# A decoder step on one core: the first doubling level of a triangular inverse as VectorE products, and a new order of the steps around it

## Time and profile before

| | before |
|---|---|
| median of 3 runs | 1878.42 us (1875.55 to 1878.49) |
| the profiled execution | 1879.94 us, span 1878.2 us |
| TensorE busy, share of the span | 1542.3 us, 82% |
| VectorE busy | 648.0 us, 35% |
| ScalarE busy | 304.9 us, 16% |
| GpSimd busy | 63.6 us, 3% |
| bytes from HBM | 499.87 MB, 271 GB/s over the span |

### The profile page before, as it was taken

The page is one execution under the profiler, slowest core; times in us unless marked ns, Lnnn a source line. Parts: engine busy times, 40 slices in busy tenths (PEclk is TensorE's granted clock), DMA queues, the critical chain, the costliest instruction groups (busy, mean ns, idle before and its releaser), DMA issues.

```text
span 1878.2 us, 24556 instructions
## 1 busy us (share of the span) xinstructions
PE 1542.3 (82%) x8870; PEld 880.0 (47%) x8870; DVE 648.0 (35%) x1288; ACT 304.9 (16%) x704; POOL 63.6 (3%) x103
## 2 busy tenths in 40 slices
PE   7999999999999999999996675666757667576574
PEld 4676767676767676767752231222312223122121
DVE  6746565656565656410121120111201112010013
ACT  2323232323232323100112000000000000000012
POOL 1101010101010101000000000000000000000000
PEclk9999999999999999999997887888878888788787
DMA  7323232323232323374589999999999999999995
GB/s 286 109 100 113 92 120 82 120 82 120 82 120 82 120 82 120 110 292 165 204 373 426 429 426 429 429 428 428 429 428 427 429 429 429 427 429 430 428 403 212
DMA packets 71904, 510.35 MB, mean 272 GB/s; under 512 B 20496, under 2 KB 23696, under 8 KB 37808
## 3 DMA queue, kind: packets, MB, share of 16 engines
q1 hardware_dynamic: 71808, 509.60, 67.2%
q0 software_dynamic: 48, 0.12, 0.0%
HBM read 499.87 MB, written 9.82 MB: 271 GB/s over the span
## 4 chain that ended last, share of the span: by engine, by line
PE 41%; DMA 34%; DVE 16%; issue 4%; ACT 2%; SPq 1%; DVEq 1%; ACTq 0%
DMA arena<-w_up 22%; DVE arena L1424 16%; DMA arena<-w_down 12%; PE ps_PJ L723 11%; PE ps_C L1069 8%; PE ps_PJ L923 7%; ACT arena L1152 2%; SPq L560 1%; PE ps_C L1120 1%; PE ps_SB L1120 1%; PE ps_YB L1120 1%; PE ps_RT L1120 1%; PE ps_C L696 0%; PE ps_PJ L1023 0%; PE ps_SB L852 0%
## 5 line engine op out<-in xcount | busy, mean ns | idle before, releaser
L723 PE MATMUL ps_PJ<-arena 128*128 128x320 f32 x1792 | 536.6, 437 | 0.0
L1069 PE MATMUL ps_C<-arena 128*32 128x512 f32 x2048 | 285.1, 719 | 178.4 <-DMA arena<-w_gate 110.3
L723 PEld LDWEIGHTS ps_PJ<-arena 128*128 128x128 f32 x1792 | 324.7, 190 | 124.6 <-issue 17.9
L1424 DVE TENSOR_TENSOR arena<-arena,ps_PJ 128x512 f32<-128x512 f32 (+2 forms) x112 | 73.5, 657 | 614.7 <-PE ps_PJ L1023 495.3
L1069 PEld LDWEIGHTS ps_C<-arena 128*32 128x32 f32 x2048 | 79.3, 130 | 377.4 <-issue 375.0
L1152 ACT ACTIVATE arena<-arena 32x160 f32<-32x160 f32 (+9 forms) x350 | 146.6, 419 | 322.0 <-DVEq L422 134.7
L1424 DVE TENSOR_TENSOR arena<-arena 128x512 f32<-128x512 f32 (+12 forms) x311 | 161.8, 520 | 73.5 <-ACTq L422 41.2
L1152 ACT ACTIVATE arena<-ps_C 128x128 f32<-128x128 f32 (+3 forms) x68 | 27.4, 403 | 893.2 <-PE ps_C L1069 530.7
L923 PE MATMUL ps_PJ<-arena 128*128 128x320 f32 x512 | 142.4, 433 | 1.0 <-DVEq L422 1.0
L923 PEld LDWEIGHTS ps_PJ<-arena 128*128 128x128 f32 x512 | 95.5, 190 | 40.2 <-issue 3.3
L1424 DVE TENSOR_TENSOR arena<-ps_PJ,arena 128x512 f32<-128x512 f32 x32 | 22.1, 692 | 258.0 <-PE ps_PJ L1016 257.9
(11 more groups left out here) (181 smaller groups left out, 1175.7 us busy)
## 6 DMA issues: line engine op xcount, KB each, us to landing
arena<-w_down SPq DMA_DIRECT2D x64, 2048.0 KB, 21.5
arena<-w_gate SPq DMA_DIRECT2D x61, 2048.0 KB, 20.4
arena<-w_up SPq DMA_DIRECT2D x61, 2048.0 KB, 20.1
arena<-win SPq DMA_DIRECT2D x59, 1024.0 KB, 4.8
arena<-w_out SPq DMA_DIRECT2D x16, 1024.0 KB, 7.0
arena<-w_gate SPq DMA_DIRECT2D x6, 1024.0 KB, 8.0
arena<-xT SPq DMA_DIRECT2D x8, 640.0 KB, 7.4
arena<-s_ret SPq DMA_DIRECT2D x8, 512.0 KB, 3.8
```

What stands on the lines that cost most here:

```text
L723: last = mm(pj(j)[:, 0:T], wt[j % NSLOT][:, kt, :], hT[:, kt, :], start=kt == 0, stop=kt == KT - 1)
L1069: last = mm((GB, UB)[u][h * CAP:(h + 1) * CAP, :], xg[:, kt, h * CAP:(h + 1) * CAP], w[h](k), start=kt == 0, stop=kt == KT - 1)
L1424: ins = build(*args)
```

## The change

- Level 1 leaves TensorE. `k1`, `i1` and `j1` and their banks go. In their place `u0` does level 1 with VectorE products: with the mask of level 1 (`Am[0]`) and `Vc`, two row shuffles inside each group of four, two products and two additions on single columns and pairs of columns, and the sum of both. Then come the transposition and `spread` as before. `u0` now also waits for the first product of `am`.
- `am` on GpSimd does the mask of level 1 first, then the two masks of the short sequences, then levels 2 to 4. All six products now wait for `ax`; the counts of `lmk` follow.
- `us0` stands ahead of `u0`, in part 0 of tile q, instead of behind `cv` in part 1.
- The moves of ScalarE get names of their own, `mb`, `mx`, `mv`. `mb` stands where it stood; the others come later: `rqb` stands behind `k3 i3` and ahead of `mx`, `xv` on VectorE behind `j3` and `mv` behind the evacuation of tile kr.

```diff
 PLAN:
-    "q": "@v ax am -va u0 | cv us0 | | k1 i1 | zs1 xb | j1 pd | ds1 | k2 i2",
-    "kr": "@q | rqa j2 zs2 xk | | rqb k3 i3 | ds2 xv | j3 | | k4 i4",
-    "vr": "@kr | rka j4 rs0 | | rkb k5 i5 -pr | ts vt | j5 rs1 | tkk -pw |",
+    "q": "@v ax am -va us0 u0 | cv | | | zs1 xb mb | pd | ds1 | k2 i2",
+    "kr": "@q | rqa j2 zs2 xk | | k3 i3 rqb mx | ds2 | j3 xv | | k4 i4",
+    "vr": "@kr mv | rka j4 rs0 | | rkb k5 i5 -pr | ts vt | j5 rs1 | tkk -pw |",
 
 buffers:
+        rows4, pair4 = cut(3200, 128, c=NC), inv[:, 1536:1600].rearrange("p (g e) -> p g e", e=2)
 
 TensorE:
                 elif s[0] == "k":
-                    pe.wait_ge(inverse, 2 * (INNER * p + int(s[1])) - 1)
+                    pe.wait_ge(inverse, 2 * ((INNER - 1) * p + int(s[1]) - 1) - 1)
 ...
 ScalarE:
-                elif s in ("xb", "xk", "xv"):
-                    x = tok[:, "vbk".index(s[1]), :, :]
-                    act.wait_ge(done("tr"), 3 * p + 1 + "bkv".index(s[1]))
+                elif s in ("mb", "mx", "mv"):
+                    x = tok[:, ("mv", "mb", "mx").index(s), :, :]
+                    act.wait_ge(done("tr"), 3 * p + 1 + ("mb", "mx", "mv").index(s))
 ...
 VectorE, u0:
+            third_row = [i // 4 * 4 + 2 for i in range(32)]
+            second_row = [i // 4 * 4 + (1 if i % 4 == 0 else 2) for i in range(32)]
 ...
                     TT(Vc[:, :, :], Ac[:, :, :], inner[0][:, None, :].broadcast_to([P, NC, BK]), ALU.mult)
                     TT(Vc[:, :, :], Vc[:, :, :], unit[:, None, :].broadcast_to([P, NC, BK]), ALU.add)
+                    x1, v1, sx = by_four(Am[:, 0, :, :]), by_four(Vc), by_four(rows4)
+                    SHUF(rows4[:, :, :], Vc[:, :, :], third_row)
+                    dve.wait_ge(lmk, (INNER + 1) * p + 1)
+                    TT(pair4[:, :, 0:1], x1[:, :, 2:3], sx[:, :, 3:4], ALU.mult)
+                    TT(x1[:, :, 3:4], x1[:, :, 3:4], pair4[:, :, 0:1], ALU.add)
+                    SHUF(rows4[:, :, :], Am[:, 0, :, :], second_row)
+                    TT(pair4[:, :, :], sx[:, :, 2:4], v1[:, :, 1:2].broadcast_to([P, BK, 2]), ALU.mult)
+                    TT(x1[:, :, 2:4], x1[:, :, 2:4], pair4[:, :, :], ALU.add)
+                    TT(Vc[:, :, :], Vc[:, :, :], Am[:, 0, :, :], ALU.add)
                     TR(Uc.rearrange("p c j -> p (c j)"), Vc.rearrange("p c j -> p (c j)")).then_inc(inverse, 1)
                     spread(Ud, Uc).then_inc(inverse, 1)
 ...
 GpSimd, am:
                     wait_freed(pool, "g4", p)
+                    pool.wait_ge(done("ac"), 2 * p + 1)
+                    TT(Am[:, 0, :, :], Ac[:, :, :], inner[1][:, None, :].broadcast_to([P, NC, BK]), ALU.mult).then_inc(lmk, 1)
                     for k in range(1, 3):
                         TT(As[:, k - 1, :], GM[:, NC, 0:P], lvlT[k], ALU.mult).then_inc(lmk, 1)
-                    pool.wait_ge(done("ac"), 2 * p + 1)
-                    for k in range(1, INNER):
+                    for k in range(2, INNER):
                         TT(Am[:, k - 1, :, :], Ac[:, :, :], inner[k][:, None, :].broadcast_to([P, NC, BK]), ALU.mult).then_inc(lmk, 1)
```

More of the change, by code:

```diff
@@ L89 @@
 LATE = {"u1": 1, "s1": 2, "u2": 1, "r2": 2, "a2": 2, "s2": 2, "r3": 2, "a3": 2, "s3": 4, "mu": 3, "va": 7}
-UNSEEN = ("xb", "xk", "xv", "ts", "pk", "ck", "cr", "cv", "e3", "lo", "sq", "pc", "pe", "p1", "p2", "ps", "b1", "b1k", "b1l", "b2a", "b2b", "ax", "am", "u0", "us0", "vt", "mk", "pd", "pr", "pw", "rqa", "rqb", "rka", "rkb", "th", "mr", "mg", "my")
+UNSEEN = ("xb", "xk", "xv", "mb", "mx", "mv", "ts", "pk", "ck", "cr", "cv", "e3", "lo", "sq", "pc", "pe", "p1", "p2", "ps", "b1", "b1k", "b1l", "b2a", "b2b", "ax", "am", "u0", "us0", "vt", "mk", "pd", "pr", "pw", "rqa", "rqb", "rka", "rkb", "th", "mr", "mg", "my")
 def schedule(now, late):
@@ L761, in step @@
                     k = int(s[-1])
-                    pe.wait_ge(lmk, (INNER + 1) * p + k)
+                    pe.wait_ge(lmk, (INNER + 1) * p + 1 + k)
                     if k == 1:
@@ L777, in step @@
                     k = int(s[1])
-                    pe.wait_ge(inverse, 2 * (INNER * p + k))
+                    pe.wait_ge(inverse, 2 * ((INNER - 1) * p + k - 1))
                     if k < INNER:
@@ L1258, in step @@
                     last.then_inc(done("ac"), 1)
-                elif s in ("k1", "k2", "k3", "k4"):
+                elif s in ("k2", "k3", "k4"):
                     wait_filled(act, s, p)
@@ L1441, in _, with by_four @@
             swapped = [i ^ 1 for i in range(32)]
+            third_row = [i // 4 * 4 + 2 for i in range(32)]
+            second_row = [i // 4 * 4 + (1 if i % 4 == 0 else 2) for i in range(32)]
+            def by_four(x):
+                return x.rearrange("p c (g e) -> p (c g) e", e=4)
             FILL(eps[:, 0:1], NORM_EPS)
@@ L1616, in step @@
                     TR(Us, V[:, NC, :]).then_inc(done("us"), 1)
-                elif s in ("i1", "i2", "i3", "i4"):
+                elif s in ("i2", "i3", "i4"):
                     wait_filled(dve, s, p)
                     spread(Zd, bank(s)[:, 0:P].rearrange("p (b j) -> p b j", b=NB32)).then_inc(free(s), 1)
-                elif s in ("j1", "j2", "j3", "j4"):
+                elif s in ("j2", "j3", "j4"):
                     wait_filled(dve, s, p)
```

## The result

| | before | after |
|---|---|---|
| median of the runs | 1876.94 us (16 runs) | 1881.12 us (16 runs) |
| after over before | | 1.0025, 95% interval 1.0017 to 1.0032 |
| profiled execution, span | 1879.94 us, 1878.2 us | 1880.7 us, 1878.9 us |

A forecast was written before the change was run, and what follows sets the result against it. The chain through VectorE and ScalarE from `@v` to `i4` bounds the pair loop: +1.58 - 0.97 = +0.61 us a pair, +4.6 us over 7.5 pairs on the 1878.42 us median. Forecast 1883.0 us, range 1873 to 1888.

The forecast's parts named there:

- The chain, not TensorE, sets the time: From `@v` to `i4`, VectorE and ScalarE set each pair's time, now 21.52 us; TensorE's work there is filler.
- TensorE's saving lost at `j2`: TensorE's own work shrinks 1.49 us a pair, but it then waits some 2.3 us at `j2` for ScalarE.
- First part, `@v` to the end of `xb`: VectorE's stretch up to `xb`: 7.73 us in place of 6.15, 1.58 longer.
- meetings: VectorE products colliding with GpSimd's, 0.22 us each; 0.65 us taken for the first part, bounds 0 to 1.3.
- Second part, `xb` to the end of `xk`: ScalarE's moves and copies, then VectorE up to `xk`: unchanged at 8.68 us.
- Third part: From `xk` to `i4`, 6.69 us before: `xv` behind `j3` gives back 0.97 us a pair.
- The sum: Pair loop: +1.58 - 0.97 = +0.61 us a pair, from -0.04 to +1.3; +4.6 us over 7.5 pairs.
- TensorE's saving counts: Rival: first part under 7.1 us shrinks the chain, up to 2.6 us a pair, 1858 us; chance 0.13.
- No change: Rival: meetings cost nothing or products fall into GpSimd's pauses, -0.04 to +0.3 a pair, 1878 to 1880.5; chance 0.30.
- Worse: Rival: every product meets, and GpSimd's `ts` products lie on `j4`'s `spread`; +1.2 a pair, 1887.5 us; chance 0.12.

The follow-up runs named there:

- 6: Changed kernel with three more 128x320 matmuls, results unused, ahead of `j2` on TensorE: 1878.70 us, 1.0015 to the kernel before.
- 7: Changed kernel with `mb` and `pd` on ScalarE moved behind `k2` and the evacuation of q: 1855.67 us, 0.9887 to the kernel before.
- 5: Changed kernel with GpSimd's short-sequence masks ahead of `ax` and its masks of levels 2 to 4 behind `xb`: 1875.70 us, 1.0000 to the kernel before.
- 2: Kernel before, level 1 on TensorE, with the new order of fillers and moves but `us0` at its old place: 1869.68 us, 0.9969.
- 3: Changed kernel with the old order of `rqb`, `xv` and the moves, `us0` still ahead of `u0`: 1888.13 us, 1.0060 to the kernel before.
- 4: Changed kernel with GpSimd's short-sequence masks ahead of `ax`, masks of levels 2 to 4 behind `u0`'s transposition: 1881.76 us, 1.0028 to the kernel before.
- 8: Kernel before, level 1 on TensorE, new filler order, `us0` at its old place, `mb` and `pd` behind q's evacuation: 1868.33 us, 0.9961.

## Why the prediction was right

- *The chain, not TensorE, sets the time.* Right, and shown by runs rather than by the trace alone: filling TensorE's wait with work costs nothing (6), and moving two steps on ScalarE is worth 25 us (7). It holds for the pairs at full clock; in the three others TensorE comes to `i4` last and does not wait there. The prediction speaks of two places where TensorE waits for VectorE in every pair. The same view has a third, L758 (`g4`, ahead of `@v`), 3.5 us over seven waits; the change leaves it at 2.9, so the sum does not hang on it.
- *TensorE's saving lost at `j2`.* I forecast a wait of 2.3 us ended by ScalarE; it is 2.06 us in five of the seven pairs behind the first and 2.35 in the last two.
- *First part, `@v` to the end of `xb`: 7.73 us.* It is 7.56, or 7.84 in two pairs. Without meetings it is 7.16 (5), against my 7.08. So the meetings take 0.40, or 0.68 in the last two pairs; I had counted 0.65 for all. Three of them catch VectorE, as I had counted, but at 0.21, 0.14 and 0.04 and not at 0.22 each. What differs in the last two pairs is who comes first where both engines start within 0.01 us of each other (which of them does is not to be told from the recorded starts): in five pairs VectorE's second product of `us0` keeps its 0.29, in the last two GpSimd's wins and it takes 0.59 or 0.60.
- *Second part, `xb` to the end of `xk`: 8.68 us.* It is 8.80 in six pairs and 9.04 in pair 1.
- *Third part: 5.72 us, 0.97 less than before.* It is 5.57 (366.93 to 372.50) in pairs at full clock; experiments 2 and 3 give 1.0 a pair from both sides.
- *The sum: +0.61 a pair.* In pairs at full clock it is +0.44, or +0.73 where the meetings cost more (`i4` is 21.94 or 22.23 behind `@v`, where it was 21.50). Here the step was too big by the 0.25 of the meetings in five pairs of seven.
- *What was left out: the clock.* In three pairs the half clock behind `j2` adds some 0.7 us, 2.1 in all (6). I had forecast the wait of 2.3 us that brings this about, and read the granted clock of 1.00 as given. A term too large and a term that was missing about cancel: that the forecast of +4.6 lies so close to the measured +4.2 is luck in part.
- *The rivals.* "TensorE's saving counts" put the turning point at a first part of 7.1 us. With 7.16 and no fall of the clock (5) the change was level with before, not faster: what kept TensorE's saving from counting was the chain through ScalarE. With ScalarE's order changed as well (7) the saving counts, and the 1855.67 us are near the 1858 of that rival. "No change" fell on the meetings, which cost 0.40 us, and on the clock. The meeting that "Worse" feared came: `ts` starts 25.1 us behind `@v` in place of 22.3, and the three products that begin with `j4`'s `spread` take 1.0 us longer (before, then after, one pair each):

```profile
281.75 1.86 DVE L1424 TENSOR_TENSOR arena<-arena 128x512 f32<-128x512 f32 x3 [0.25 <-DVE arena L1424]
376.23 2.84 DVE L1425 TENSOR_TENSOR arena<-arena 128x512 f32<-128x512 f32 x3 [0.24 <-DVE arena L1425]
```

TensorE still does not wait at `i5`, so the meeting costs nothing, as the argument against this rival had it.

The rule on the shared port (the Trainium skill, SBUF — State Buffer, section "Who interferes with whom") is borne out further than I used it. It lists copies, where they run in a two-port mode, among the VectorE operations that can collide with GpSimd. In experiment 4 a copy of `cv` did (its two copies took 0.69 us in place of 0.47); in which mode it ran, no trace shows. A transposition (0.32 beside a product of GpSimd, in the changed kernel at 351.38) did not.

## What to carry to other kernels

Work taken off the busiest engine is worth only what the chain of waits gives back: look which queue the next consumer stands behind, and move the steps there that nobody waits for yet; here two names moved in a list turned a loss of 4 us into a gain of 21. Price a new sequence of small operations by their rows and add the meetings with an engine that shares a port, and ask what a longer wait does to the clock. When an experiment moves a collision or a wait, look at what stands at the new place before reading its time.

## What the runs showed of the hardware

- The granted clock fell to the lower level behind waits of TensorE of 2.05 to 2.34 us in a loop in which it is busy 96 us of 100, and not always: in three of seven pairs of the changed kernel, and in three of seven in experiments 3 and 4 as well, though not in the same pairs. Behind waits of 0.45 us (6) and 1.0 us (5) in the same place it fell in none of seven pairs. In pair 0, at 62 us, TensorE waits 2.1 us at `g4` in all eleven profiles, and the clock fell there in five (experiments 2, 3, 4, 6 and 8). What decides between two equal waits stays open.
- A shuffle of 128x128 takes 0.30 us where the prediction had taken 0.32. A product of 128x32 with a step of four elements takes 0.22, against 0.19 for the one of that size in the earlier trace rows; one of 128x64 with the same step takes 0.23, against 0.225 for the one there, which reads PSUM. So the step costs 0.03 us or less here.
- Whether VectorE or GpSimd wins a near tie repeats over pairs, and then flips for the rest of an execution: the same code took 7.56 us in five pairs and 7.84 in the last two of the changed kernel's profile, and 7.56 in all seven in that of experiment 6.
